# A three-stage transformer forward pass on one core: the routing and the token gather of the expert stage rewritten, the last expert team's down product in pairs, and the final normalisation moved inside that team

## The chip, the cores and the metric

The kernel runs on one core of a Trainium2 chip. The metric is the device time of one execution in microseconds (us), the median of repeated runs. The engines are named as the profile names them: PE (TensorE, matmul; PEld its weight loads), DVE (VectorE), ACT (ScalarE), POOL (GpSimd), SP (SyncE, which here issues almost all DMAs).

## The reference

256 tokens of width 1024, all in float32. Two blocks run one after the other; the change touches only the end of the second.

```python
x = first_block(x, ...)                 # attention / state space mixer, 2 layers, dense FFNs
x = x + mixer(rmsnorm(x, g_mix), ...)   # gated linear attention and block attention
x = x + memory_attention(...)           # cross attention to a memory of 256 tokens
x = x + hier_moe(rmsnorm(x, g_moe), ...)
return rmsnorm(x, g_final)

def hier_moe(h):                        # 32 experts in 4 groups of 8, D_EXPERT = 512
    g_prob = softmax(h @ w_rg + b_rg)               # one group for each token
    p_grp, grp = top_k(g_prob, 1)
    e_in = (h @ w_re + b_re) of that group          # 8 logits
    top_p, top_i = top_k(softmax(e_in), 2)          # two experts for each token
    weights = p_grp * top_p / sum(top_p)
    for each chosen expert e:
        out[token] += ((silu(x @ w_gate[e]) * (x @ w_up[e])) @ w_down[e]) * weight
```

Each expert has 6 MiB of weights (gate and up 1024 x 512, down 512 x 1024), all 32 together 192 MiB, and all of them are read, whatever the routing is.

## The kernel before

Every engine has its own hand-written program (`sync`, `gpsimd`, `scalar`, `tensor`, `vector`), and they meet through semaphores. `X` [128, 2, 1024] holds the residual, with 128 tokens of each of two token blocks (`tb`) on the partitions. All stages before the expert stage split weights and tokens in two parts and take three matmuls for one product (L1259 to L1261); the change doesn't touch them.

**Routing.** After the last output product of the memory attention, DVE adds the residual (`add_residual(5)`). `norm(7)` on PE turns raw `X` by 16 transposes (L1135). DVE and ACT empty two banks each into `HT` (`norm_columns(7)`, L1795 and L718). ACT then squares and sums the rows (`norm_sq(7)`, L710), DVE takes the inverse root in 11 small dependent operations (`rsqrt`, L1766 to L1771) and writes the normed tokens `XN` (L1783). PE makes the 36 router logits from `HT` (L1629). DVE chooses group and experts (L2453 to L2481; a lambda `both` does each step for one token block and then the other), giving `mAS`, which marks the two chosen experts of each token. PE sums `mAS` over tokens (L1638 to L1642), the rank of a token within its expert. DVE meanwhile makes the weights (L2485 to L2493), then from the ranks the slot numbers `mRK` and the number of rounds (L2498 to L2504, semaphore `ranked`). An expert has 32 slots (`SLOTS`); if an expert had more than 32 tokens the whole loop over the experts would be run again (`rounds`; it is 1 here). PE runs filler transposes (`ROUTE_FILLERS`, L1634 and L1754) between these.

**The expert stage.** Experts go in 8 teams of 4. `choose` (DVE, L2516 and L2521) makes `mS`, a 0/1 matrix tokens x (4 experts x 32 slots), and `mSW`, the same with the weights. `gather` (PE, L1649) takes `XN[:, tb, kt::KT]` as the stationary operand, a column stride of 8 elements, and `mS` as the moving one: its 16 matmuls (32 records of the profile, since a float32 matmul has two) give the chosen tokens, turned. ACT and DVE empty four 128-column pieces each into `mGT`. `gate_or_up` (L1697) and `down` (L1718) take a weight slab as the moving operand, and each expert uses 32 columns of the array, so that four run side by side. `turn_hidden` (L1708) turns the hidden values. After `down`, ACT and DVE copy a half each of the result to `mY` (L1101, L2547), and PE scatters it back to the tokens with `mSWT` (L1746, 4 matmuls), and DVE adds to `X` (L2555). Within `team`, PE looks ahead: the gather of the next team stands between `down` and the scatter.

**The transfers.** A piece is 1 MiB, half a matrix of one expert: 24 pieces a team, 192 in all. SP issues them in program order into a ring of 12 slabs. For the first team there are 9 places more (`EXTRA`, buffers that have become free elsewhere), so 21 pieces go out before any expert has been computed. The last of these goes over `HT` and waits for the router logits. Every other piece waits in `put` for the count `piece_used`, which PE raises by 4 each time it has finished a half of gate, up or down (`pay` puts the increment on the next matmul of another phase). The piece after the first 21 therefore waits for the first half of the first team's gate product.

**The end.** `over_teams` runs team 0 (peeled on some engines), a loop, and the last team, then reads the number of rounds from SBUF into a register (`value_load`) and branches. After that ACT squares `X` (`norm_sq(8)`), DVE takes the roots, scales `X` into `XN` (L1783) and multiplies by the gain (L2573), and SP writes each token block out (L600).

## Time and profile before

| what | value |
|---|---|
| median of 3 runs | 1436.96 us (1435.53 to 1438.4) |
| the profiled execution, its own time | 1435.04 us |
| its span, first to last instruction | 1433.3 us |
| mean granted TensorE clock | 0.936 |
| busy in the span: PE, PEld, DVE, ACT, POOL | 1220.0, 965.1, 682.6, 462.5, 27.2 us |
| DMA, mean over the span | 240 GB/s, 343.94 MB |

"Busy" is the time in which an engine executes; a busy engine need not be the one that the end waits for. The expert stage starts near 950 us and runs to the end. Whoever reads this profile has to look at that stage apart from the first two thirds, since its limit is another one.

### The profile page before, as it was taken

What the parts mean: (1) busy time and instruction counts of PE and PEld (TensorE: products, weight loads), DVE (VectorE), ACT (ScalarE), POOL (GpSimd) and SP (SyncE); (2) the same over time, 40 slices, a digit from 0 to 9 for tenths busy, and PEclk for the clock granted to TensorE, in tenths of its full rate; (3) what the DMA queues carried; (4) which work ended last, traced back from release to release, by engine and by line L of the source; (5) the groups of instructions that cost most, each with busy time, mean ns of one, the idle gap of its engine ahead of it and who ended that gap; (6) DMA issues with size and microseconds to landing.
All of it is one profiled execution on the core that took longest, in us unless ns stands there. A gap on an engine that the chain in (4) does not pass through costs nothing. (4 is left out here: it accounts for less than half of the span.)

```text
span 1433.3 us, 19994 instructions
## 1 busy us (share of the span) xinstructions
PE 1220.0 (85%) x8216; PEld 965.1 (67%) x8216; DVE 682.6 (48%) x1012; ACT 462.5 (32%) x588; POOL 27.2 (2%) x83
## 2 busy tenths in 40 slices
PE   6899999999998999999998899989784866748664
PEld 5786999998986999998896897875331332314221
DVE  7987475557777575557355766651110101101012
ACT  6366344325564443325352544411100100101000
POOL 2210000000000000000000000000000000000000
PEclk9899999999999999999995999999997888988897
DMA  9423365554433365556450455876999999999993
GB/s 263 76 83 118 113 227 192 190 189 151 166 109 109 122 226 190 191 176 195 136 177 30 147 177 167 341 300 251 422 420 422 422 422 422 422 421 422 422 421 148
DMA packets 137145, 343.94 MB, mean 240 GB/s; under 512 B 9826, under 2 KB 99036, under 8 KB 112500
## 3 DMA queue, kind: packets, MB, share of 16 engines
q1 hardware_dynamic: 135276, 337.96, 63.0%
q0 software_dynamic: 1696, 4.99, 1.9%
q8 instruction: 50, 0.82, 0.2%
q14 instruction: 19, 0.16, 0.0%
q10 hardware_dynamic: 104, 0.02, 0.0%
HBM read 340.32 MB, written 2.62 MB: 239 GB/s over the span
## 5 line engine op out<-in xcount | busy, mean ns | idle before, releaser
L1259 PE MATMUL ps<-HT_hi,piece_hi 128*128 128x256 f32 x1088 | 310.4, 285 | 7.2 <-DVE HT_lo L1875 4.3
L1884 DVE TENSOR_TENSOR piece_lo<-ring,piece_hi 128x2048 fp32r<-128x2048 f32 x118 | 266.9, 2286 | 87.5 <-ACT piece_hi L766 86.8
L1260 PE MATMUL ps<-HT_lo,piece_hi 128*128 128x256 f32 x1088 | 308.3, 283 | 0.0
L1261 PE MATMUL ps<-HT_hi,piece_lo 128*128 128x256 f32 x1088 | 308.1, 283 | 0.0
L766 ACT ACTIVATE piece_hi<-ring 128x2048 fp32r<-128x2048 f32 x118 | 222.9, 1911 | 195.1 <-PE ps L1261 160.1
L1259 PEld LDWEIGHTS ps<-HT_hi,piece_hi 128*128 128x128 f32 x1088 | 209.0, 192 | 10.7 <-issue 7.8
L1260 PEld LDWEIGHTS ps<-HT_lo,piece_hi 128*128 128x128 f32 x1088 | 209.2, 192 | 0.8
L1261 PEld LDWEIGHTS ps<-HT_hi,piece_lo 128*128 128x128 f32 x1088 | 209.1, 192 | 0.0
L1697 PE MATMUL ps<-ring,arena 128*32 128x512 f32 x992 | 137.7, 712 | 67.9 <-DMA ring<-in_w_exp_up_dram 66.8
L1697 PEld LDWEIGHTS ps<-ring,arena 128*32 128x32 f32 x992 | 36.9, 128 | 162.8 <-issue 161.5
L1718 PE MATMUL ps<-ring,arena 128*32 128x512 f32 x472 | 76.4, 798 | 56.3 <-DMA ring<-in_w_exp_down_dram 56.3
L1718 PEld LDWEIGHTS ps<-ring,arena 128*32 128x32 f32 x472 | 21.5, 139 | 103.0 <-issue 103.0
L2547 DVE COPY arena<-ps 128x512 f32<-128x512 f32 x8 | 5.5, 692 | 143.8 <-PE ps L1718 143.8
L2545 DVE TENSOR_TENSOR arena<-arena,ps 128x512 f32<-128x512 f32 x8 | 5.5, 688 | 141.4 <-PE ps L1697 141.4
L1259 PE MATMUL ps<-piece_hi,HB_hi 128*128 128x512 f32 x176 | 69.7, 396 | 0.0
L1260 PE MATMUL ps<-piece_lo,HB_hi 128*128 128x512 f32 x176 | 69.5, 395 | 0.0
L1261 PE MATMUL ps<-piece_hi,HB_lo 128*128 128x512 f32 x176 | 69.4, 394 | 0.0
L1649 PEld LDWEIGHTS ps<-arena,XN 128*128 128x128 f32 x256 | 61.7, 335 | 8.6 <-issue 8.6
L1649 PE MATMUL ps<-arena,XN 128*128 128x128 f32 x256 | 63.2, 407 | 2.0 <-DVE arena L2521 2.0
L1259 PE MATMUL ps<-piece_hi,HT_hi 128*128 128x256 f32 (+1 forms) x192 | 58.2, 303 | 1.2 <-PE ps L1261 1.2
L1260 PE MATMUL ps<-piece_lo,HT_hi 128*128 128x256 f32 (+1 forms) x192 | 57.7, 301 | 0.0
L1261 PE MATMUL ps<-piece_hi,HT_lo 128*128 128x256 f32 (+1 forms) x192 | 57.7, 301 | 0.0
(451 smaller groups left out, 1711.5 us busy)
## 6 DMA issues: line engine op xcount, KB each, us to landing
ring<-in_w_exp_gate_dram SPq DMA_DIRECT2D x64, 1024.0 KB, 18.6
ring<-in_w_exp_up_dram SPq DMA_DIRECT2D x60, 1024.0 KB, 15.8
ring<-in_w_exp_down_dram SPq DMA_DIRECT2D x59, 1024.0 KB, 15.9
ring<-in_ffn_w_gate_dram SPq DMA_DIRECT2D x22, 1024.0 KB, 5.6
ring<-in_ffn_w_up_dram SPq DMA_DIRECT2D x22, 1024.0 KB, 5.4
ring<-in_ffn_w_down_dram SPq DMA_DIRECT2D x22, 1024.0 KB, 7.3
ring<-in_w_in_dram SPq DMA_DIRECT2D x20, 1024.0 KB, 5.3
ring<-in_odd_w_in_dram SPq DMA_DIRECT2D x12, 1024.0 KB, 5.2
```

The lines of the kernel that those rows point to most:

```text
L766: act.activation(piece_hi[:, h % HI_SLABS, :], ring[:, k % RING, :], ACT.Copy).then_inc(hi_made, 1)
L1259: pe.matmul(out, sh, mh, start=start, stop=False, skip_group_check=True)
L1260: pe.matmul(out, sh, ml, start=False, stop=False, skip_group_check=True)
L1261: return pe.matmul(out, sl, mh, start=False, stop=stop, skip_group_check=True)
L1649: ins = pe.matmul(ps[:, kt // 4, (kt % 4) * P:(kt % 4 + 1) * P], XN[:, tb, kt::KT], mS[:, tb, :], start=(tb == 0), stop=(tb == 1))
L1697: ins = pe.matmul(ps[own, 2 + up, :], mGT[:, kt, own], w[e][:, k4, :], start=(kt == 0), stop=(kt == KT - 1))
L1718: ins = pe.matmul(ps[own, 4 + c, :], mHT[:, 2 * half + f, own], w[e][:, f, c * 512:(c + 1) * 512], start=(half == f == 0), stop=(half == f ...
L1884: ve.tensor_tensor(piece_lo[k % RING][:, :], ring[:, k % RING, :], piece_hi[:, h % HI_SLABS, :].bitcast(F32), ALU.subtract).then_inc(split, 1)
L2545: ve.tensor_tensor(mH, mG, up, ALU.mult).then_inc(m_hid, 1)
L2547: ve.tensor_copy(mY[:, 512:1024], ps[:, 5, :]).then_inc(m_y["v"], 1)
```

## The change

Ahead of the expert stage:

- ACT squares before it empties its half of `norm7`; it also writes `XN` itself, in an order in which the 128 columns that one gather matmul takes lie side by side. DVE no longer writes `XN` at this place.
- The two token blocks' logits are two PSUM tiles of 36 columns, made in turn, as `HT`'s pieces come. The choice on DVE treats both blocks in one instruction where the instruction allows it. The slot numbers count from 1, so that one operation goes.
- `choose` is one operation for `mS` and one for `mSW`. The first `gather` waits for `mS` alone. The number of rounds is counted after the first `choose`.
- The first gather is made in halves: kt 0 to 3, then the first half of gate, then kt 4 to 7. `mGT` is signalled piece by piece. In all teams `gather` reads contiguous columns.
- Fillers go from 60 and 28 to 22 and 6. POOL makes its constants and issues the load of the final gain earlier (after `c_o` instead of after the norm).

At the end:

- `value_load` of the rounds stands ahead of the last team on every engine.
- In the last team, the second `down` half goes by pairs of experts (0, 1 and 2, 3), each with its own waits. In all teams the two column halves are finished one after the other and signalled apart, the scatter goes by column halves.
- Squares, roots, and scaling stand in the last team: ACT squares each block as soon as it is added, DVE multiplies block 1 by the gain meanwhile, and after the roots DVE scales block 0 and ACT block 1. The result lies in `MT`.

```diff
-ROUTE_FILLERS = 60, 28
+ROUTE_FILLERS = 22, 6
@@ over_teams
+                if isinstance(before, int):
+                    eng.wait_ge(ranked, 1)
+                    count = eng.value_load(rounds_i[0:1, :], min_val=1, max_val=T // SLOTS)
                 team(before + (TEAMS - 1), TEAMS - 1, False)
-            one_round(0)
-            eng.wait_ge(ranked, 1)
-            rounds = eng.value_load(rounds_i[0:1, :], min_val=1, max_val=T // SLOTS)
+            rounds = one_round(0)
@@ gpsimd
-            pool.wait_ge(normed, 16)
+            pool.wait_ge(bank_full, full_count("c_o", 1))
@@ scalar
+            norm_sq(7, X)
             norm_columns(7)
-            norm_sq(7, X)
+            act.wait_ge(rt_root, 1)
+            for tb in range(2):
+                act.activation(XN[:, tb, :].rearrange("p (k c) -> p c k", k=KT),
+                               X[:, tb, :].rearrange("p (c k) -> p c k", k=KT), ACT.Copy,
+                               scale=ms[:, 32 + tb:33 + tb]).then_inc(normed, 1)
...
+                else:
+                    for tb in range(2):
+                        act.wait_ge(m_added[tb], g + 2)
+                        ins = act.activation(final_sq[:, tb * D:(tb + 1) * D], X[:, tb, :], ACT.Square, scale=1.0 / 32,
+                                             accum_out=ms[:, 16 + tb:17 + tb])
+                    ins.then_inc(m_sq, TEAMS)
+                    act.wait_ge(m_root, g + 1)
+                    act.activation(result[1], result[1], ACT.Copy, scale=ms[:, 35:36]).then_inc(m_gained, TEAMS)
@@ tensor
+            def gather(g, halves, pay=lambda ins: None):
-                pe.wait_ge(m_sel, g + 1)
-                for kt in range(KT):
-                    for tb in range(2):
-                        ins = pe.matmul(ps[:, kt // 4, (kt % 4) * P:(kt % 4 + 1) * P], XN[:, tb, kt::KT],
-                                        mS[:, tb, :], start=(tb == 0), stop=(tb == 1))
+                pe.wait_ge(m_pick, g * 2 + 2)
+                for half in halves:
+                    for k4 in range(4):
+                        kt = 4 * half + k4
+                        for tb in range(2):
+                            ins = pe.matmul(ps[:, half, k4 * P:(k4 + 1) * P], XN[:, tb, kt * P:(kt + 1) * P],
+                                            mS[:, tb, :], start=(tb == 0), stop=(tb == 1))
...
+                        if half == up == 0 and isinstance(g, int) and g == 0:
+                            gather(g, (1,))
+                            turn(g)
...
+                    for experts in (((0, 1), (2, 3)) if half and not look else (range(TEAM),)):
+                        w = {e: take(2) for e in experts}
                         for c in range(2):
-                            for e in range(TEAM):
...
+                            if half and e == TEAM - 1:
+                                ins.then_inc(m_y_full, 1)
...
-                pe.wait_ge(m_y["a"], g + 1)
-                pe.wait_ge(m_y["v"], g + 1)
-                for tb in range(2):
-                    for half in range(2):
+                for half in range(2):
+                    pe.wait_ge(m_y["av"[half]], g + 1)
...
+                    for tb in range(2):
                         ins = pe.matmul(ps[:, 2 + 2 * tb + half, :], mSWT[:, tb * P:(tb + 1) * P],
@@ vector
                 if not look:
                     ve.wait_ge(m_added[0], g + 2)
                     ve.wait_ge(m_added[1], g + 2)
-                    ve.nop()
+                    ve.tensor_tensor(result[1], X[:, 1, :], gfin, ALU.mult).then_inc(m_finished, TEAMS)
+                    ve.wait_ge(m_sq, g + 1)
+                    ve.wait_ge(m_finished, g * 2 + 2 - TEAMS)
+                    rsqrt(ms[:, 16:18], ms[:, 34:36])
+                    ve.nop().then_inc(m_root, TEAMS)
+                    ve.scalar_tensor_tensor(result[0], X[:, 0, :], ms[:, 34:35], gfin, ALU.mult, ALU.mult)\
+                        .then_inc(m_finished, TEAMS)
```

How the instructions stand on PE where the expert stage begins. The names: `router_w` are the router's weights, `ident` the identity of the fillers and transposes, `arena` holds the choosing matrices, the ranks' operands and the gathered tokens, `ring` is expert weights. Before:

```order
L1629 MATMUL ps<-router_w,HT 128x36 x16
L1634 MATMUL ps<-ident 128x128 x60
L1642 MATMUL ps<-arena 128x32
L1754 MATMUL ps<-ident 128x128 x28
L1649 MATMUL ps<-arena,XN 128x128 x16
L1657 MATMUL ps<-ident,arena 128x128 x2
L1697 MATMUL ps<-ring,arena 32x512 x48
```

After:

```order
L1651 MATMUL ps<-router_w,HT 128x36 x16
L1657 MATMUL ps<-ident 128x128 x22
L1665 MATMUL ps<-arena 128x32
L1790 MATMUL ps<-ident 128x128 x6
L1674 MATMUL ps<-arena,XN 128x128 x8
L1728 MATMUL ps<-ring,arena 32x512 x16
L1674 MATMUL ps<-arena,XN 128x128 x8
L1683 MATMUL ps<-ident,arena 128x128 x2
L1728 MATMUL ps<-ring,arena 32x512 x32
```

The first half of gate (16 matmuls) now has 8 gather matmuls ahead of it instead of 16 and two transposes. (Four of the five rank matmuls are left out in both.)

DVE in the middle of the choice, from the comparison that marks the group to the last operation on `mAS`, all of it on small tiles in `arena`. Before:

```order
L2465 TENSOR_SCALAR arena<-iota,arena 128x4 x2
L2466 TENSOR_SCALAR arena<-arena 128x8 x2
L2468 SCALAR_TENSOR_TENSOR arena<-arena 128x8 x6
L2470 MAX arena<-arena 128x8 x2
L2471 MAX_INDEX arena<-arena 128x8 x2
L2473 TENSOR_TENSOR arena<-arena 128x1 x2
L2474 CAST arena<-arena 128x2 x2
L2476 TENSOR_SCALAR arena<-iota,arena 128x8 x2
L2477 TENSOR_SCALAR arena<-iota,arena 128x8 x2
L2478 TENSOR_TENSOR arena<-arena 128x8 x2
L2481 TENSOR_SCALAR arena<-arena 128x8 x8
```

After:

```order
L2501 TENSOR_TENSOR arena<-iota,arena 128x2x4
L2504 TENSOR_TENSOR arena<-arena 128x2x32
L2506 TENSOR_REDUCE arena<-arena 128x2x8
L2486 MAX arena<-arena 128x8 x2
L2489 MAX_INDEX arena<-arena 128x8 x2
L2508 TENSOR_TENSOR arena<-arena 128x2
L2509 TENSOR_SCALAR arena<-arena 128x2
L2510 CAST arena<-arena 128x2x2
L2518 TENSOR_TENSOR arena<-iota,arena 128x2x16
L2520 TENSOR_TENSOR arena<-arena 128x2x8
L2521 TENSOR_TENSOR arena<-arena 128x64
```

32 instructions have become 13.

DVE at the end of the last team, from the copy of `mY` on (`TENSOR_LOAD` is the read of the number of rounds). Before:

```order
L2547 COPY arena<-ps 128x512
L2555 TENSOR_TENSOR X<-X,ps 128x512 x4
L417 TENSOR_LOAD arena
L417 ISA x2
L418 COMPARE_AND_BRANCH
```

After, where the next eleven rows are the root, as before:

```order
L419 TENSOR_LOAD arena
L419 ISA x2
L2580 TENSOR_TENSOR arena<-arena,ps 128x512
L2583 TENSOR_TENSOR arena<-arena,ps 128x512
L2585 COPY arena<-ps 128x512
L2594 TENSOR_TENSOR X<-X,ps 128x512 x4
L2600 TENSOR_TENSOR MT<-X,final_gain 128x1024
L1802 TENSOR_SCALAR ms<-ms 128x2
```

The read has moved ahead of the last team; the gain's product follows the adds directly.

## Rows read from the trace of the kernel before

**Rows 1.** the page, rate of the DMAs in 40 slices of 35.8 us
```profile
GB/s 263 76 83 118 113 227 192 190 189 151 166 109 109 122 226 190 191 176 195 136 177 30 147 177 167 341 300 251 422 420 422 422 422 422 422 421 422 422 421 148
```

**Rows 2.** stretches of all engines: us, busy times, PEclk, DMA share, GB/s
```profile
960.00:965.00 5.00, 4.33 (x40) 4.10 (x39) 4.69 (x35) 0.00 (x0) 0.00 (x0) 1.00 0.02 7
990.00:1400.00 410.00, 283.74 (x1686) 124.02 (x1682) 46.42 (x102) 31.53 (x63) 0.00 (x0) 0.87 1.01 422
```

**Rows 3.** SP's issues of expert pieces around the gap: start, length, count
```profile
952.41 0.33 SPq L504 DMA_DIRECT2D HT<-in_w_exp_down_dram  x1
980.54 1.29 SPq L517 DMA_DIRECT2D ring<-in_w_exp_down_dram  x3
```

**Rows 4.** PE in order of time, routing and first team
```profile
948.64 3.73 PE L1629 MATMUL ps<-router_w,HT 128*128 128x36 f32 x32 [0.97 <-DVE HT L1795]
952.21 8.41 PE L1634 MATMUL ps<-ident 128*128 128x128 f32 x60
967.66 7.88 PE L1649 MATMUL ps<-arena,XN 128*128 128x128 f32 x32 [1.98 <-DVE arena L2521]
976.84 10.51 PE L1697 MATMUL ps<-ring,arena 128*32 128x512 f32 x96 [1.07 <-ACT arena L1083]
```

**Rows 5.** DVE in order of time, norm, choice, slots
```profile
952.82 1.42 DVE L1783 TENSOR_SCALAR XN<-X,ms 128x1024 f32<-128x1024 f32 x2
...
954.16 0.21 DVE L2455 SCALAR_TENSOR_TENSOR arena<-ps,ms,router_b 128x4 f32<-128x4 f32 x1
...
960.07 1.16 DVE L2481 TENSOR_SCALAR arena<-arena 128x8 f32<-128x8 f32 x8
...
964.68 0.23 DVE L2498 SCALAR_TENSOR_TENSOR arena<-ps,arena 128x64 f32<-128x64 f32 x1
...
966.50 0.49 DVE L2516 TENSOR_TENSOR arena<-arena 128x128 f32<-128x128 f32 x2 [0.62 <-DVE arena L2504]
```

**Rows 6.** ACT in order of time, squares, exponentials, first gathered pieces
```profile
949.48 1.05 ACT L710 ACTIVATE XN<-X 128x1024 f32<-128x1024 f32 x1
...
958.91 0.30 ACT L1077 ACTIVATE arena<-arena 128x4 f32<-128x4 f32 x1 [8.30 <-DVE arena L2473]
...
975.64 1.14 ACT L1083 ACTIVATE arena<-ps,cols 128x128 f32<-128x128 f32 x4 [15.87 <-PE ps L1649]
```

**Rows 7.** a stretch of 1 us in the routing, for the PE clock
```profile
953.00:954.00 1.00, 1.00 (x7) 1.00 (x6) 1.00 (x2) 0.00 (x0) 0.00 (x0) 0.50 1.02 418
```

**Rows 8.** weight loads by form: busy, mean ns
```profile
L1649 PEld LDWEIGHTS ps<-arena,XN 128*128 128x128 f32 x256 | 61.7, 335 | 8.6 <-issue 8.6
...
L1619 PEld LDWEIGHTS ps<-arena 128*128 128x128 f32 x16 | 3.0, 190 | 0.4
```

**Rows 9.** the last two pieces: issues, and us to landing
```profile
L517 SPq DMA_DIRECT2D ring<-in_w_exp_down_dram x2: 429/430/430, 1385.6 to 1386.1; - x2
DMA to landing us min/median/max: 21.1/22.1/23.0
```

**Rows 10.** PE at the end: last down half, scatter
```profile
1399.34 5.34 PE L1718 MATMUL ps<-ring,arena 128*32 128x512 f32 x32 [2.99 <-DMA ring<-in_w_exp_down_dram]
...
1409.27 5.34 PE L1718 MATMUL ps<-ring,arena 128*32 128x512 f32 x32 [4.59 <-DMA ring<-in_w_exp_down_dram]
...
1415.52 3.67 PE L1746 MATMUL ps<-arena 128*128 128x512 f32 x8 [0.91 <-DVE arena L2547]
```

**Rows 11.** the chain that ended last, from the last add on
```profile
1420.60 0.55 DVEq L417
...
1424.09 0.18 DVE ms L1766
...
1426.25 1.43 DVE XN L1783 x2
...
1427.71 1.23 DVE XN L2573
```

**Rows 12.** SP's last issue
```profile
1430.10 0.34 SPq L600 DMA_DIRECT2D out_dram<-XN  x1
```

More of the change, by code:

```diff
@@ L1738, in team @@
                 if look:
-                    gather(g + 1, pay)
+                    gather(g + 1, (0, 1), pay)
                 pe.wait_ge(m_swt, g + 1)
-                pe.wait_ge(m_y["a"], g + 1)
-                pe.wait_ge(m_y["v"], g + 1)
-                for tb in range(2):
-                    for half in range(2):
+                for half in range(2):
+                    pe.wait_ge(m_y["av"[half]], g + 1)
+                    if half and owed:
+                        pe.nop().then_inc(piece_used, TEAM)
+                    for tb in range(2):
                         ins = pe.matmul(ps[:, 2 + 2 * tb + half, :], mSWT[:, tb * P:(tb + 1) * P],
                                         mY[:, half * 512:(half + 1) * 512], start=True, stop=True)
-                        pay(ins)
-                    ins.then_inc(m_out_full, 1)
+                        ins.then_inc(m_out_full, 1)
                 if look:
@@ L2436, in _ @@
             add_residual(5)
+            route = rt.rearrange("p (b c) -> p b c", b=2)
+            o.mark(ve.memset(route[:, :, 36:40], NEG))
             norm_columns(7)
             norm(7, X)
-            rb = full_tile(ve, "router", 0)
-            qs = [rt[:, 128 * tb:128 * tb + 128] for tb in range(2)]
-            def both(*steps):
-                for step in steps:
-                    for q in qs:
-                        o.mark(step(q))
-                ve.wait_ge(v_order, o.count)
@@ new lines, in _ @@
+            logits = route[:, :, 0:32].rearrange("p b (g e) -> p b g e", g=N_GROUPS)
+            in_group, group_is = route[:, :, 96:104], route[:, :, 56:60]
+            for tb in range(2):
+                o.mark(ve.scalar_tensor_tensor(rt[:, 128 * tb:128 * tb + 36], full_tile(ve, "router", tb)[:, 0:36],
+                                               ms[:, 32 + tb:33 + tb], router_b[:, :], ALU.mult, ALU.add))
+            ve.wait_ge(v_order, o.count)
+            ve.nop().then_inc(emptied["v"], 2)
```

241 lines of the change are left out of this document (124 added, 117 removed).

## The prediction, written before the changed kernel ran

> **What bounds the kernel now.** First the rate of the transfers over the whole span [rows 1]. In the first two thirds it goes up and down with the stages. From slice 29 on it stands at 422 GB/s until the end. Ahead of that there is a hole: from 960 to 965 us the DMAs move almost nothing [rows 2], and from 990 to 1400 us they are busy without a break at 422 GB/s, while PE is busy for 284 of 410 us. So the expert stage waits for weights and not for PE.
>
> The hole is explained by SP's issues [rows 3]. The piece over `HT` goes out at 952.41, the next one at 980.54: all 21 places are full, and SP waits for the first half of the first gate product. After that issue 171 pieces of 1.049 MB follow, 179.3 MB, at 422 GB/s 425 us; with a few us of start-up that is 1409, and the last piece lands at 1386.1 + 23.0 = 1409.1 [rows 9], whereupon PE starts at 1409.27 [rows 10]. The end therefore consists of three parts: the time of the issue at 980.54, a stream of fixed length, and what comes after the last landing (1433.3 - 1409.2 = 24.1 us). The change can't shorten the stream. It can move its start and shorten its end.
>
> **The front: from the logits to the issue.** Now [rows 4 to 6]: logits finished at 952.2, DVE first writes `XN` (952.82 to 954.16), chooses until 961.23 (the end of L2481), weights until 964.68, slots until the gather starts at 967.66; gather 7.88 us, turn, `mGT`, gate at 976.84, issue 3.70 us later.
>
> - Start of the choice. The squares no longer wait behind ACT's two banks, and `XN` goes to ACT, so the root is done before the logits are. The choice starts at about 952.3, 1.9 us earlier. Were the root no earlier than now, it would be 952.8; ACT's banks come a bit later, which may hold the logits up by some 0.5 us. Both are in the range.
> - The choice. Now 46 instructions take 7.07 us. After it there are 20: five steps done twice (0.24 to 0.4 us a pair) make 1.8 us, ten single ones make 1.8 us, since a dependent small one costs 2.16/11 = 0.20 (the root from 1424.09 to 1426.25, [rows 11]) and one of 64 columns 0.23 [rows 5]. Together 3.6 us, end at 955.9: 3.5 saved. An operation with a broadcast in four dimensions isn't in these rows; I bound it by 0.16 and 0.49/2 us, which over seven of them is -0.3 and +0.3 us.
> - Exponentials, weights, ranks. ACT's four small instructions (0.30 us the longest, [rows 6]) start at about 955.3 and end at 956.2. Six weight operations are 1.3 us (now 3.45): 957.5. PE's 22 fillers start at 952.2. At the full clock's 3.73/32 = 0.117 us a record [rows 4] they would end at 954.8, at half of it all along at 957.3. At 953 the granted clock is 0.50, the 1.2 GHz level [rows 7], and the 60 fillers now took 8.41 us, 0.14 each, so partly half: I take 956.2. Ten rank records, 1.2 us: 957.4. They just meet the weights.
> - Slots: 0.23 + 0.4 us, since one operation and the counting of rounds go behind the choosers. Gather at 958.35 instead of 967.66: 9.3 us earlier so far.
> - The first gather. Now 32 records take 7.88 us, 0.246 each, with loads of 335 ns; contiguous loads of the same size take 190 ns [rows 8], and the router's 32 records, with contiguous stationary operands, ran at 0.117. Sixteen records by that are 1.9 us (by today's pace 3.9). Then one `mGT` piece, 0.37 us with its wait (four take 1.14, [rows 6]). Gate starts at 960.7 rather than 976.84; this part is 2.35 us where it was 9.18, so 6.8 saved. The other half of gather and the turn, 2.2 us, stand behind the first gate half. They delay only PE, which has slack: ring pieces are used in 3.5 us a group and arrive in 9.9.
>
> The Trainium skill ("TensorE: Matmul & The Clock Gate", section on LDWEIGHTS) says that the time of a weight load depends on its columns alone. By that rule the new layout would change nothing in the gather, and the sum would be 2.0 us smaller. The loads of 335 against 190 ns disagree, with 128 columns in both.
>
> Front: 1.9 + 3.5 + 3.9 + 6.8 = 16.1 us. The issue moves from 980.54 to 964.4. The earlier pieces end near 961 [rows 2, 3], so the hole shrinks from about 20 us to 3.5 and all of the 16.1 passes into the stream. No more than 20 can be had here. SP's queue has no new wait ahead of the issue. POOL's load of the gain (0.5 MB, 1.2 us of transfer) moves to a time when pieces flow; none of them is needed before gate's first half is done, so nothing.
>
> **The tail: from the last landing (called L, 1409.2).** The last two pieces land 2.4 us apart (1385.6 + 21.1, 1386.1 + 23.0, [rows 9]), so the first pair is there at L - 4.9. PE is busy with the other down half until 1404.68 [rows 10].
>
> - Pairs. 96 records, four side by side, took 10.51 us [rows 4], 0.44 a step at full clock; the 32 at 1409.27, after a wait of 4.6 us, took 5.34, partly half clock. A pair has 8 steps: 1404.7 to 1408.2, then L to L + 3.5. The break of 1 us is like the one ahead of 976.84, after which the pace was full. Saved 1.9.
> - Copies lie under the second column half, so the scatter (3.67) follows at once, and one add of about 0.7 is left after it: last add at L + 7.9. Now it ends at 1420.5, L + 11.3. Saved 3.4 with the pairs.
> - Squares: block 0's starts with its own add, block 1's ends 1.6 us after the last add, L + 9.5 (now L + 14.8, since reading the rounds and branching stand between, 1420.60 and 0.55 us of it, and two squares of 1.05 follow). The root's 2.16 stays: L + 11.8 with its waits. The gain's product of block 1 is hidden under the squares.
> - One fused pass, about 1.25 us, on both engines, where 1.43 + 2 x 1.23 stand now [rows 11]; then branch and wait, 0.4: both outputs go at L + 13.4. Now L + 19.8 and L + 20.9 [rows 12], and 3.2 us after the second issue is the end. Two together share the DMAs: 0.35 for the second issue and 0.9 more for its bytes. End at L + 17.9 or so, against 24.1: 6.1 us.
>
> Reading the rounds ahead of the last team costs some 0.8 us on each engine where all of them wait for weights. SP runs far ahead there: its pieces take 21 to 23 us from issue to landing [rows 9].
>
> Sum: 16.1 + 6.1 = 22.2. The profiled execution had 1435.04 us with a span of 1433.3: 1411.1 span, 1412.8 own time. The median lies 1.9 above it: 1436.96 - 22.2 = **1414.8**.
>
> **Rivals.**
>
> - *Half clock where the stream waits.* PE had the half clock at 953 [rows 7]. Should it have it in the first gather and the first gate half, these take 1.9 + 3.5 us more: 1420.2. For it: less filler work stands before. Against it: the gate at 976.84 ran at full pace after a gather and a break.
> - *The gather's pace isn't the load's.* Then the first half takes 3.9: 1416.8.
> - *ACT becomes the routing's bound.* It now squares, empties two banks, writes `XN` with each element 128 apart, and only then comes to the exponentials. At 1.05 us each, as the contiguous pass [rows 6], `XN` is ready at 952.6, 2.7 us before it matters. From 2.4 us each on, each us counts. At four times the price (4.2 each) the exponentials end 3.6 later: 1418.4. No strided write of this size stands in the rows, so this is open. The Trainium skill ("SBUF — State Buffer", in the section on the DMA port swizzle) says that accesses that each go to another 16-byte line pay a penalty. The load of 335 ns above fits that; what ACT pays no row shows.
> - *The front's gain is lost,* since the stream would have another limit behind the hole: only the tail counts, 1430.9. Against it: 422 GB/s without a dip over 410 us.
> - *Nothing changes:* a new wait takes both gains. I see no place that costs 22 us.
> - *Slower: the ring runs dry in every team.* The two halves of the team (columns apart, scatter by halves, waits by piece) hold back `piece_used`. Four pieces give the DMAs 9.9 us, PE needs 5.34 for a group even with a half clock. A release must come about 4.6 us later than now before the DMAs stop. To eat 22.2 + 2.9 us over seven teams it must be 4.6 + 3.6 = 8.2 us later in each. The gather in the loop gets shorter, by up to 4 us, so it speaks against it.
>
> **How the numbers follow.** Forecast 0.63; half clock 0.13; gather's pace 0.07; ACT 0.07; front lost 0.04; nothing 0.03; slower 0.03. The forecast by itself has 1411 to 1418: choice and banks -1 to +2, fillers and ranks -1.3 to +2.3, tail with half clock +3, hole fully closed -3.5. With the half clock and ACT the range is 1410.5 to 1421.5, and some 1 in 10 lie above it. A measurement tells 0.2%, 2.9 us, from no change. Faster 0.94, same 0.03, slower 0.03.
>
> **What would show it.** The first issue after the `HT` piece at about 964.4, and the hole's end with it. The gather's records at 0.12 instead of 0.246 us. `XN` by ACT at 1.05 us each. 422 GB/s through the stream, and the last landing at about 1393. After it some 18 us to the end, with the last 16 down records in 3.5. Wrong it would be if the rate between 970 and 1390 had dips, if the clock at the first gate was 0.5, or if the exponentials came after 957.

## The result and the profile after

| | before | after |
|---|---|---|
| median of 4 runs each | 1436.24 us (1435.06 to 1438.4) | 1411.51 us (1410.73 to 1412.85) |
| span of the profiled execution | 1433.3 | 1409.3 |
| its mean granted clock | 0.936 | 0.929 |

The ratio is 0.9827, with a 95% interval of 0.981 to 0.9844: 24.7 us less, where 22.2 had been forecast. A later group of runs gave 1413.07 us (1410.81 to 1415.3) for the same changed kernel, 21.9 us less than the 1434.92 us of the kernel before in that group. So the difference between two medians wanders by 2.8 us, more than the 2.5 us between forecast and measurement.

First the rate of the DMAs in 40 slices, on the page of the changed kernel, against [rows 1]:

```profile
GB/s 261 83 85 120 92 221 192 191 189 183 146 108 115 118 209 180 183 190 223 158 151 90 120 135 193 297 338 337 421 422 422 422 421 421 423 422 421 423 420 217
```

Then the same in stretches around the hole (length, busy times of PE, PEld, DVE, ACT and POOL, PEclk, DMA share, GB/s), against [rows 2]:

```profile
955.00:960.00 5.00, 4.15 (x37) 3.08 (x40) 2.00 (x9) 1.14 (x4) 0.00 (x0) 1.00 0.41 170
960.00:965.00 5.00, 4.68 (x43) 2.70 (x36) 0.50 (x2) 0.28 (x1) 0.00 (x0) 1.00 0.28 70
965.00:1385.00 420.00, 282.05 (x1786) 103.07 (x1790) 48.27 (x96) 33.51 (x66) 0.00 (x0) 0.83 1.01 422
```

The hole in the stream is still there, but it lasts from about 957 to 963.5 instead of from about 960 to 981. Behind it the stream has the same 422 GB/s, and PE still has a third of its time free (282 of 420 us busy). SP's issues around the hole, in order of time, show why; they answer to [rows 3]:

```profile
950.07 0.33 SPq L510 DMA_DIRECT2D HT<-in_w_exp_down_dram  x1
962.53 1.28 SPq L523 DMA_DIRECT2D ring<-in_w_exp_down_dram  x3
```

From one issue to the next it was 28.1 us and is now 12.5. The program between them, on PE, in order of time, against [rows 4]:

```profile
946.30 3.73 PE L1651 MATMUL ps<-router_w,HT 128*128 128x36 f32 x32 [0.39 <-issue]
949.87 2.60 PE L1657 MATMUL ps<-ident 128*128 128x128 f32 x22
953.97 0.41 PE L1661 MATMUL ps<-arena 128*128 128x32 f32 x2 [1.50 <-DVE arena L2521]
...
956.21 2.02 PE L1674 MATMUL ps<-arena,XN 128*128 128x128 f32 x16 [0.24 <-DVE arena L2556]
958.84 3.64 PE L1728 MATMUL ps<-ring,arena 128*32 128x512 f32 x32 [0.61 <-ACT arena L1095]
962.41 2.05 PE L1674 MATMUL ps<-arena,XN 128*128 128x128 f32 x16
```

On DVE, start of the choice, its end, and the slots, against [rows 5]:

```profile
949.85 0.48 DVE L2495 SCALAR_TENSOR_TENSOR arena<-ps,ms,router_b 128x36 f32<-128x36 f32 x2 [1.42 <-PE ps L1651]
...
953.70 0.22 DVE L2521 TENSOR_TENSOR arena<-arena 128x64 f32<-128x64 f32 x1
...
955.31 0.23 DVE L2535 SCALAR_TENSOR_TENSOR arena<-ps,arena 128x64 f32<-128x64 f32 x1
955.63 0.43 DVE L2556 TENSOR_TENSOR arena<-arena 128x256 f32<-128x256 f32 x1
```

On ACT, `XN` and the first exponential, against [rows 6]:

```profile
948.52 3.94 ACT L1082 ACTIVATE XN<-X,ms 128x1024 f32<-128x1024 f32 x2 [1.59 <-DVEq L1815]
953.20 0.30 ACT L1088 ACTIVATE arena<-arena 128x4 f32<-128x4 f32 x1 [0.74 <-DVEq L2511]
```

The weight loads of the gather, grouped by form (busy time, mean ns), against [rows 8]:

```profile
L1674 PEld LDWEIGHTS ps<-arena,XN 128*128 128x128 f32 x256 | 29.3, 192 | 7.2 <-issue 7.2
```

The end, all engines in order of time with the weight loads left out, against [rows 10] and [rows 12]:

```profile
1391.63 3.63 PE L1753 MATMUL ps<-ring,arena 128*32 128x512 f32 x16 [1.32 <-DMA ring<-in_w_exp_down_dram]
...
1395.18 3.70 PE L1783 MATMUL ps<-arena 128*128 128x512 f32 x8
...
1398.92 0.69 DVE L2594 TENSOR_TENSOR X<-X,ps 128x512 f32<-128x512 f32 x1 [0.17 <-PE ps L1783]
...
1400.79 0.19 ACT L1119 ACTIVATION_READ_ACCUMULATOR HT<-X 128x1 f32 x1
...
1403.38 1.28 DVE L2605 SCALAR_TENSOR_TENSOR MT<-X,ms,final_gain 128x1024 f32<-128x1024 f32 x1 [0.16 <-DVE ms L1807]
1404.96 0.83 SPq L606 DMA_DIRECT2D out_dram<-MT  x2
```

**How to compare two such traces.** The stages ahead of the expert stage are the same program in both, but they don't end at the same time. The first residual add ahead of the routing, on DVE, starts at 941.15 before and at 939.40 after. In the 13 profiled executions of this study it started anywhere from 938.15 to 941.67, and in the two of the changed kernel at 939.40 and 938.15. So I measure the front from the start of that add (called R) to the first issue of a piece after the hole (called the issue), the stream from the issue to the start of the last down products, and the tail from these. "The issue at R + 23.13" means 23.13 us after R. In the table the tail's rows are the time from the start of the last down products to the last add's end, the start of the last root and the end of the span.

| part | before | after | gained | forecast |
|---|---|---|---|---|
| R to the start of the choice | 13.01 | 10.45 | 2.56 | 1.9 |
| the choice (to the end of `mAS`) | 7.07 | 4.07 | 3.00 | 3.5 |
| to the gather (exponentials, weights, ranks, slots) | 6.43 | 2.29 | 4.14 | 3.9 |
| gather to gate | 9.18 | 2.63 | 6.55 | 6.8 |
| gate to the issue | 3.70 | 3.69 | 0.01 | 0 |
| the stream, issue to the last down products | 428.73 | 429.10 | -0.37 | 0 |
| from there to the last add's end | 11.23 | 7.98 | 3.25 | 3.4 |
| ... to the start of the last root | 14.82 | 9.46 | 5.36 | 5.3 |
| ... to the end | 24.03 | 17.67 | 6.36 | 6.1 |

Front 16.26, stream -0.37 and tail 6.36 make 22.25. R's 1.75 us are the rest of the 24.0 us between the spans (1433.3 - 1409.3).

### The profile page after: what moved, and what is told of

It reads as the page before. It is cut to its first block, busy times and chain, and to the rows that moved or that the text cites. A ratio compares the mean times of both kernels' runs of the same rounds, so it can differ in the third digit from the quotient of the medians.

```text
span 1409.3 us, 19857 instructions
## 1 busy us (share of the span) xinstructions
PE 1192.3 (85%) x8156; PEld 926.1 (66%) x8156; DVE 674.5 (48%) x948; ACT 467.7 (33%) x591; POOL 28.9 (2%) x83
## 4 chain that ended last, share of the span: by engine, by line
PE 59%; DMA 23%; DVE 9%; ACT 4%; issue 3%; SPq 2%; POOL 0%; DVEq 0%; ACTq 0%; POOLq 0%
PE ps L1279 15%; PE ps L1280 14%; PE ps L1281 14%; DMA ring<-in_w_exp_down_dram 11%; DMA ring<-in_w_exp_up_dram 11%; PE ps L1728 4%; PE ps L1753 3%; DVE piece_lo L1923 1%; SPq L523 1%; PE ps L1195 1%; DVE arena L2271 1%; ACT piece_hi L772 1%; PE ps L1383 1%; PE ps L1155 1%; DVE arena L1872 1%
## 5 line engine op out<-in xcount | busy, mean ns | idle before, releaser
L1728 PE MATMUL ps<-ring,arena 128*32 128x512 f32 x992 | 149.6, 759 | 85.5 <-DMA ring<-in_w_exp_up_dram 64.3
L1728 PEld LDWEIGHTS ps<-ring,arena 128*32 128x32 f32 x992 | 40.9, 134 | 187.1 <-issue 186.6
L1753 PE MATMUL ps<-ring,arena 128*32 128x512 f32 x472 | 80.3, 800 | 47.0 <-DMA ring<-in_w_exp_down_dram 47.0
L1753 PEld LDWEIGHTS ps<-ring,arena 128*32 128x32 f32 x472 | 21.5, 142 | 98.1 <-issue 98.1
L1110 ACT ACTIVATE arena<-ps 128x512 f32<-128x512 f32 x8 | 4.8, 597 | 162.2 <-PE ps L1742 162.2
L1944 DVE TENSOR_TENSOR arena<-ps,arena 128x512 f32<-128x512 f32 x22 | 15.2, 692 | 84.4 <-PE ps L1281 84.3
```

Source lines behind the costliest of these rows:

```text
L1728: ins = pe.matmul(ps[own, 2 + up, :], mGT[:, kt, own], w[e][:, k4, :], start=(kt == 0), stop=(kt == KT - 1))
L1753: ins = pe.matmul(ps[own, 4 + c, :], mHT[:, 2 * half + f, own], w[e][:, f, c * 512:(c + 1) * 512], start=(half == f == 0), stop=(half == f ...
L1944: ve.tensor_tensor(by_token(G), by_token(gate), roots[1 + 2 * layer][1].unsqueeze(1).to_broadcast([P, 2, T]), ALU.mult).then_inc(gate_scal ...
```

## The experiments

Each group of runs had its own runs of the kernel before, with medians of 1436.42 (first four kernels), 1436.36 (next four) and 1434.92 (last three). Each ratio is against these. Edits are shown against the changed kernel, except the first. Where the text speaks of the changed kernel's 1411.51 us or of R + 23.13, it means the runs and the profile of the result. The changed kernel's own medians differ by 1.6 us from group to group, so for smaller effects the profiles carry the argument.

**1. The tail alone (tail_only).** The kernel before, with the change's edits behind the last landing only: pairs, copies and scatter by halves, `value_load` ahead of the last team, squares and gain inside it. For instance:

```diff
-            one_round(0)
-            eng.wait_ge(ranked, 1)
-            rounds = eng.value_load(rounds_i[0:1, :], min_val=1, max_val=T // SLOTS)
+            rounds = one_round(0)
@@ scalar, and so in the other places of the end
-            norm_sq(8, X)
+            act.nop().then_inc(fin[1], 1)
```

> The kernel before with only the end of the change: the rounds read ahead of the last team, the last down half in pairs, scatter by column halves, squares and scaling in the last team. Theory A (fixed stream between a front and a tail, which add): no change up to the last landing, then 17.7 us to the end where the kernel before has 24.0, so 6.3 us faster, near 1430. Theory B (the end gains only because the front also moved, or the extra reads and waits in the loop cost something): less than 4 us faster, and a rate under 422 GB/s in the stream.

Measured: 1429.59 us (1428.8 to 1431.43), ratio 0.9949 [0.9932, 0.9966], 6.8 us less than its runs of before. In its profile R is at 941.20 and the issue at R + 41.1, against R + 39.4 in the kernel before, since the first gate product took 12.20 us against 10.51 in [rows 4]: the clock was at 0.50 from 977 to 980. From the issue to the end of the last add are 437.1 us, as in the changed kernel (1399.61 - 962.53). From the issue to the end it is 447.4 where the kernel before has 452.8 and the changed one 446.8. So the tail is worth 5.4 us by the profiles and 6.8 by the medians (forecast 6.1), as theory A said, and the rest belongs to the front.

**2. Gather with the old stride (strided).**

```diff
-                act.activation(XN[:, tb, :].rearrange("p (k c) -> p c k", k=KT),
-                               X[:, tb, :].rearrange("p (c k) -> p c k", k=KT), ACT.Copy,
+                act.activation(XN[:, tb, :], X[:, tb, :], ACT.Copy,
@@ tensor, gather
-                            ins = pe.matmul(ps[:, half, k4 * P:(k4 + 1) * P], XN[:, tb, kt * P:(kt + 1) * P],
+                            ins = pe.matmul(ps[:, half, k4 * P:(k4 + 1) * P], XN[:, tb, kt::KT],
```

> The changed kernel, with XN in its old order: ACT writes it contiguously, and the gather takes every eighth column as its stationary operand. Theory A (a weight load with a stride of 32 bytes is slower, and the front passes one to one into the end): 0.246 us a record, the first gather half 3.9 instead of 2.0 us, the issue after the gap 2 us later, the time 2 us longer; ACT's two passes at 1.05 instead of 1.97 us win nothing. Theory B (load time depends on columns alone): no change of the gather. Theory C (ACT's pass is what the routing waits for): faster, by up to 1.8 us.

Measured: 1418.67 us (1417.07 to 1420.74), ratio 0.9876 [0.986, 0.9893], 7.2 us over the changed kernel. PE in order of time around the first gather:

```profile
957.69 4.04 PE L1673 MATMUL ps<-arena,XN 128*128 128x128 f32 x16 [0.24 <-DVE arena L2555]
962.34 5.34 PE L1727 MATMUL ps<-ring,arena 128*32 128x512 f32 x32 [0.61 <-ACT arena L1094]
```

Its weight loads by form, its `XN` on ACT, and two stretches (columns as above):

```profile
L1673 PEld LDWEIGHTS ps<-arena,XN 128*128 128x128 f32 x256 | 61.8, 335 | 7.2 <-issue 7.2
```

```profile
950.04 2.19 ACT L1082 ACTIVATE XN<-X,ms 128x1024 f32<-128x1024 f32 x2 [1.62 <-DVEq L1814]
```

```profile
1000.00:1005.00 5.00, 4.88 (x23) 1.91 (x25) 4.43 (x10) 1.27 (x2) 0.00 (x0) 1.00 1.01 423
1005.00:1010.00 5.00, 5.00 (x52) 1.62 (x48) 0.10 (x1) 0.40 (x1) 0.00 (x0) 1.00 0.67 211
```

The same 16 records take 4.04 us with the stride and 2.02 without it, and in the gather nothing but the operand's address pattern differs. That is what theory A said, and it rules out theory B. The rest of the 7.2 us A did not foresee. The first half of gate took 5.34 instead of 3.64, at a granted clock of 0.62 and 0.52 between 962 and 966, and the stream had a dip to 211 GB/s at 1005 to 1010. My reading of the dip is that PE came late to the next release of ring places: it was busy for 19.9 of the 20 us from 990 to 1010. The strided gather of the next team, 32 records in 7.91 us, can't be the whole reason, for the kernel before has the same gather in the same place and no dip:

```profile
1000.15 7.90 PE L1649 MATMUL ps<-arena,XN 128*128 128x128 f32 x32
```

```profile
1015.00:1020.00 5.00, 3.71 (x36) 0.91 (x28) 0.59 (x1) 0.60 (x1) 0.00 (x0) 1.00 1.02 423
1020.00:1025.00 5.00, 3.43 (x20) 1.06 (x24) 0.10 (x1) 0.00 (x0) 0.00 (x0) 0.66 1.01 421
```

From the issue to the start of the second team's gate there are 31.1 us before (1011.64 - 980.54), 29.9 in the changed kernel (992.44 - 962.53) and 36.1 in strided (1003.80 - 967.73). What is new in strided is that the second half of the first gather, 4.10 us with the stride, now also stands behind the issue. So the dip goes with the split and the stride together; this is argued from the traces, not tried by itself. The sum is closed: R 1.48 later, gather 2.02, gate half 1.70, stream 2.14 and tail 0.06 make the 7.4 between the spans. Of the 5.9 us without R, the strided loads ahead of the issue are a third; the stream's 2.1 came later, and whether the stride has any part in the clock's fall at gate isn't shown. (Tail_only, whose gather is strided too, had the fall at the same place, the kernel before had one earlier, at 970, during its gather.) The contiguous write by ACT, 2.19 us where it was 3.94, won nothing, so theory C falls: ACT then waited 2.46 us for DVE instead of 0.74.

**3. The first gather whole (whole).**

```diff
-                if isinstance(g, int):
-                    gather(g, (0,))
-                else:
-                    gather(g, (0, 1))
-                    turn(g)
+                gather(g, (0, 1))
+                turn(g)
@@ team
-                        if half == up == 0 and isinstance(g, int) and g == 0:
-                            gather(g, (1,))
-                            turn(g)
```

> The changed kernel, with the first gather made as a whole (16 matmuls and the turn) ahead of the first gate half. Theory A: the first gate half ends 2.2 to 2.4 us later, the DMA gap is longer by that, the time 2.3 us longer. Theory B (the split is hidden by the wait for the first gathered pieces): under 1 us.

Measured: 1414.36 us (1413.56 to 1415.57), ratio 0.9845 [0.9829, 0.9862]. The issue comes at R + 24.47 instead of 23.13. So the halves are worth 1.34 us: 1.79 for the 16 other records (3.81 us for 32, 2.02 for 16) and 0.14 for the turn's transposes, less the wait of 0.61 us for ACT ahead of gate, which these records cover. That lies between the theories (2.2 to 2.4, and under 1): A left out the covered wait. The median is 2.85 us higher, but of the 3.4 us between the profiled spans 2.27 are R, at 941.67.

**4. A delay ahead of the gather (delay).** `ROUTE_FILLERS = 22, 92` instead of 22, 6.

> The changed kernel with 86 more filler transposes (92 instead of 6) between the ranks and the first gather, at 0.117 us each 10.1 us of pure delay on PE. Theory A (one to one): the issue after the gap 10 us later, the last landing 10 us later, the tail as it is, 9.8 us longer (some 0.3 us of the fillers were hidden). Theory B (slack in the stream takes part of it): less than 8 us.

Measured: 1421.98 us (1420.31 to 1424.67), ratio 0.9903 [0.9886, 0.992]. The issue is at R + 33.70, 10.57 later than in the changed kernel, and the median is 10.5 higher. From the issue to the end are 446.9 us, against 446.8. Theory A holds: the delay passes to the end one to one. Its size isn't the fillers' alone, since the clock was at 0.50 from 954 to 957.

**5 and 6. Fillers (fill_none, fill_old).** `ROUTE_FILLERS = 0, 0`, and `60, 28` as before.

> The changed kernel without any filler transposes in the routing. Theory A (the fillers hold the PE clock through the first gather and gate, and cost nothing, since PE waits for VectorE at the ranks anyway): the clock falls to the 1.2 GHz level somewhere from the ranks to the first gate, the issue after the gap comes 2 to 5 us later. Theory B (they do nothing, the later work is dense enough): gate at 19.4 us after the first residual add, as now, and no change of the time within 1 us.

> The changed kernel with the old number of fillers, 60 and 28. By 0.117 us each at full clock the 60 end at 7.0 us instead of 2.6 after the router's matmuls; PE waits 1.5 us for VectorE there now, so the ranks come 2.9 us later. The 28 instead of 6 take 2.6 us more, of which 0.2 are a wait now; the choosers are 2.9 us later too. Together 5.2 to 5.5 us later at the issue and in the time. If the clock is at half for a part, up to 8 us.

Measured: without fillers 1415.81 us (1415.75 to 1416.05), ratio 0.9858 [0.9841, 0.9874], issue at R + 25.90. With the old ones 1419.03 (1415.49 to 1420.41), ratio 0.9884 [0.9867, 0.99], issue at R + 27.43. Both cost, for opposite reasons. Without fillers the issue comes 2.8 us later, within theory A's 2 to 5. With the old ones it comes 4.3 us later, where 5.2 to 5.5 were expected: 60 fillers took 6.6 us from start to start of what follows, 0.110 each, not 0.117. PE without fillers, a stretch of it (PE alone: busy, PEclk, DMA share, GB/s) and the gather:

```profile
954.00:956.00 2.00, 0.00 (x0) 0.50 1.02 430
```

```profile
956.09 0.64 PE L1661 MATMUL ps<-arena 128*128 128x32 f32 x2 [3.94 <-DVE arena L2521]
...
959.37 3.76 PE L1674 MATMUL ps<-arena,XN 128*128 128x128 f32 x16 [0.93 <-DVE arena L2556]
```

PE waits 3.94 us for the choice, the clock falls to 0.50, the 1.2 GHz level, and ranks and gather run at that level. With 60 and 28 fillers PE has no wait at all from the router's products to the gather and the clock stays at 1.00 from 945 to 970 in this execution, but the fillers are themselves in the way:

```profile
950.07 6.75 PE L1657 MATMUL ps<-ident 128*128 128x128 f32 x60
...
957.69 3.25 PE L1790 MATMUL ps<-ident 128*128 128x128 f32 x28
```

The profiled execution was the fastest of the four; what made the other three 2.5 to 4.9 us longer no trace shows.

**7. No pairs (no_pairs).**

```diff
-                    for experts in (((0, 1), (2, 3)) if half and not look else (range(TEAM),)):
+                    for experts in (range(TEAM),):
```

> The changed kernel, the last down half in one group of four experts. Theory A: PE stands idle for 5 us ahead of the last landing and then does 32 records instead of 16, with the clock at half for a part: 5.3 instead of 3.6 us, last add 1.7 to 2 us later, the time the same. Theory B (pairs win by an earlier first column half alone): under 0.5 us, since both have 8 steps after the last landing.

Measured: 1413.77 us (1413.04 to 1417.31), ratio 0.9851 [0.9834, 0.9867]. The last down half in one piece:

```profile
1392.92 4.92 PE L1753 MATMUL ps<-ring,arena 128*32 128x512 f32 x32 [3.46 <-DMA ring<-in_w_exp_down_dram]
```

The last add ends 9.27 us after the start of these products instead of 7.98, and the end is 18.98 behind instead of 17.67: the pairs are worth 1.3 us. They don't save steps: at the full clock 32 records of a down half took 3.64 us (the first half, in the profile of whole), and the 16 of the last pair take 3.63, since both have eight steps one after the other. What they save is the clock. Without pairs PE waits 3.46 us for the landing, and the clock is at 0.50 from 1393 to 1395; with them it waits 1.32 us, and the clock is at 1.00 from 1392 to 1395. So theory A had the reason, with a price of 1.7 to 2 us that was too high, and B left the clock out. Another 1.16 us of its profiled span come from the front, where the clock fell at 955 in this execution.

**8. The number of rounds read late (late_rounds).**

```diff
             def one_round(before):
...
+                team(before + (TEAMS - 1), TEAMS - 1, False)
                 if isinstance(before, int):
                     eng.wait_ge(ranked, 1)
                     count = eng.value_load(rounds_i[0:1, :], min_val=1, max_val=T // SLOTS)
-                team(before + (TEAMS - 1), TEAMS - 1, False)
```

> The changed kernel, with the rounds read behind the last team, as before. The read was 0.55 us in the chain before, with its issue some 0.9: the outputs are issued 0.8 to 1.0 us later relative to the last landing, and nothing else moves. Rival: reading it in the loop's last turn costs PE time ahead of the last team, then this kernel is the same or faster.

Measured: 1414.97 us (1413.75 to 1415.32), ratio 0.985 [0.9834, 0.9867]. The last add ends at the same 7.98, but the outputs are issued 14.24 us after the start of the last products instead of 13.33. The read behind the team costs 0.9 us, all of it between the writing of the result and its issue, as expected; the rival falls. The rest of the median's difference is not the read's: in the profiled execution the clock fell at 951, during the router's products, so that the issue came at R + 24.67, and R itself was at 940.93.

**9. The changed kernel again (after_again).**

> The changed kernel once more, unchanged, as the measure for the other kernels of this group. Theory A (my account of the profiled pair): the change is worth 22.6 us (16.3 ahead of the stream's restart, 6.4 behind the stream), and the remaining 1.75 us of the two spans' difference lies ahead of the residual add and is scatter between executions. Then the residual add starts anywhere from 938 to 942 us in this execution, the wait of 960 us lasts to 23.1 us after it, the tail after the last down projection's start is the same to 0.1 us, and the median lies within 1411 to 1414. Theory B: the 1.75 us are a gain of the change by some effect on the earlier part: then the residual add starts at 939.4 again, within 0.5 us, where the kernels of the groups before had 938.3 to 941.7.

Measured: 1413.07 us (1410.81 to 1415.3), ratio 0.9853 [0.9836, 0.9869]. R is at 938.15, so theory B falls: the 1.75 us of the profiled pair are scatter ahead of the change. The kernels that share the changed front have R from 938.15 to 941.67, on both sides of the 941.15 before. But A's 23.1 us to the issue were not met either; it was 24.29. PE of this execution, and a stretch of it (PE alone):

```profile
948.62 2.60 PE L1657 MATMUL ps<-ident 128*128 128x128 f32 x22
952.73 0.41 PE L1661 MATMUL ps<-arena 128*128 128x32 f32 x2 [1.51 <-DVE arena L2521]
...
954.01 1.52 PE L1790 MATMUL ps<-ident 128*128 128x128 f32 x6
955.32 2.81 PE L1674 MATMUL ps<-arena,XN 128*128 128x128 f32 x16
```

```profile
954.00:956.00 2.00, 2.00 (x11) 0.50 0.87 360
```

The instructions are the same, behind the same wait of 1.5 us as in the first profile, yet here the clock went to 0.50 and cost 1.16 us. What decides between the two no trace shows.

**10. More fillers, only as many as fit (fill_34).** `ROUTE_FILLERS = 34, 6`.

> 34 filling matmuls instead of 22 ahead of the ranks, everything else as in the changed kernel. The ranks waited 1.50 us for VectorE there, and a filler took 0.117 us (22 in 2.60): 12 more take 1.4 us and end just as VectorE has the picks ready. Theory A (the time is VectorE's and the fillers only fill): issue after the gap and median within 0.3 us of the changed kernel's. Theory B (some executions of the changed kernel lose the clock in the gap, and more filling holds it): the median falls by up to 1.5 us, to about 1410, and its spread narrows. Against both: if the fillers ran at 0.19 us each, as they would at half the clock, they would end 2.3 us late and the median would be 1 to 2 us above.

Measured: 1411.36 us (1410.98 to 1413.2), ratio 0.984 [0.9826, 0.9854]. PE:

```profile
950.25 3.91 PE L1657 MATMUL ps<-ident 128*128 128x128 f32 x34
954.36 0.41 PE L1661 MATMUL ps<-arena 128*128 128x32 f32 x2 [0.20 <-DVE arena L2521]
```

The fillers end as VectorE has the marks ready, the clock stays at 1.00 from 945 to 970, and the issue comes at R + 23.13, as in the better of the changed kernel's two profiles: theory A's figure. (At half clock a filler costs more than the 0.19 us of the expectation: in late_rounds the 22 took 4.93 us, 0.22 each.) Against the changed kernel of the same group the median is 1.7 us lower; against its eight runs of both groups (median 1412.2) 0.8 us. The intervals overlap, so this version is no worse in these runs, and that it is better isn't shown.

**11. ACT's banks ahead of its squares (cols_first).**

```diff
-            norm_sq(7, X)
             norm_columns(7)
+            norm_sq(7, X)
```

> ScalarE empties its banks of turned columns before it squares, as in the kernel before; the rest is the changed kernel. The root and the strided write of XN then come later on ScalarE by the time of the bank copies, about 1 to 2 us, and the two writes last 3.94 us. In the changed kernel ScalarE ended them 0.74 us before VectorE had the arguments of the exponentials. Theory A (the routing is VectorE's; ScalarE has 0.74 us to spare): the exponentials start (delay minus 0.7) later, and with the later root of the logits' scaling the issue after the gap moves by about 1 to 1.7 us, median 1412.5 to 1413.5. Theory B (the order of the two jobs on ScalarE decides nothing, the router's products came first anyway): issue and median within 0.3 us.

Measured: 1415.88 us (1415.08 to 1416.9), ratio 0.9865 [0.985, 0.9881], issue at R + 27.01, 3.9 later: more than either theory gave. ACT and PE:

```profile
953.18 3.83 ACT L1082 ACTIVATE XN<-X,ms 128x1024 f32<-128x1024 f32 x2 [2.26 <-DVEq L1815]
956.82 0.25 ACT L1088 ACTIVATE arena<-arena 128x4 f32<-128x4 f32 x1
```

```profile
957.30 0.64 PE L1661 MATMUL ps<-arena 128*128 128x32 f32 x2 [3.06 <-DVE arena L2521]
...
960.77 3.39 PE L1674 MATMUL ps<-arena,XN 128*128 128x128 f32 x16
```

The root comes later and the choice starts 1.28 us later (first `max` at R + 12.35 instead of 11.07). Now the exponentials follow `XN` without a wait, and DVE waited 0.41 us for them instead of 0.17. But that didn't reach the end, for with the weights made DVE still had to wait for the ranks:

```profile
959.68 0.22 DVE L2535 SCALAR_TENSOR_TENSOR arena<-ps,arena 128x64 f32<-128x64 f32 x1 [0.77 <-PE ps L1665]
```

The other 2.6 us are PE: after a wait of 3.06 us the clock is at 0.50 from 957 until past 963, and from the start of the ranks to the start of gate it takes 7.48 us instead of 4.87. Of theory A's 1 to 1.7 us there are 1.28, by the later root and none by ACT's own length; what A left out was the clock.

## Why the prediction was right

The mechanism was right: the end is a front, a stream of fixed length, and a tail, and the two ends were shortened by about what was said. That the sum of the parts came out at 22.25 against 22.2 is partly luck: the four front terms were off by +0.7, -0.5, +0.2 and -0.25 us, and the misses cancel.

**The limit.** The end is the issue plus a constant. In the eight profiles of kernels which leave the stream and the tail alone (after, after_again, whole, delay, fill_none, fill_old, fill_34, cols_first) the span minus the time of the issue lies between 446.6 and 446.9 us, while the issue itself moves from 962.4 to 972.0. That confirms the step on which all rested, and rules out the rival that the front's gain is lost. Of the hole some 6.5 us are left, where the prediction had 3.5: it took the start of the hole as 961 and left it there, but transfers ended near 960 before and end near 957 now, since R came 1.75 us and the logits another 0.6 us earlier. A front gain of 10 us more would not have passed whole into the stream.

**Start of the choice.** 2.56 us instead of 1.9. I had let the logits end as before; they came 0.6 us earlier, since PE waited 0.39 us ahead of them and not 0.97 [rows 4]. The root was done 1.4 us before the logits (DVE's wait of 1.42), so it had the cover that the prediction gave it.

**Choice.** 3.00 instead of 3.5. Twenty instructions took 4.07 us and not 3.6. By start to start, the five steps done twice were 1.97 us (forecast 1.8), the ten single ones 2.10 (1.8): two of them on 64 columns took 0.26 and 0.30 with their gap, and the step behind the cast waited 0.15 us for it. The bound of +0.3 us for the broadcasts held.

**Exponentials to slots.** 4.14 instead of 3.9. The fillers had the full clock (2.60 us, not the 4.0 that I chose between the bounds of 2.6 and 5.1), so PE was not late but waited 1.50 us for the marks. This miss cost nothing, since ranks and weights ended together at 955.3, and the weights alone (1.25 us, forecast 1.3) would have held the slots until then.

**Gather.** 6.55 instead of 6.8. Its 16 records took 2.02 (forecast 1.9), and the first piece on ACT and its waits 0.61 (forecast 0.37). Experiment 2 shows that the pace belongs to the load: 335 ns with a column stride of eight elements, 192 without, with 128 columns both times. The rival "the gather's pace isn't the load's" falls with it, and so does the sum by the rule of the Trainium skill ("TensorE: Matmul & The Clock Gate", section on LDWEIGHTS), in which columns alone count.

**The tail.** 6.36 instead of 6.1; the tail alone gave 5.4 to 6.8. Inside it the pairs were over-sized: 5.34 - 3.63 = 1.7 us against the kernel before, and 1.3 against experiment 7, not 1.9. All of it is the granted clock (experiment 7): in one piece the 32 records took 5.34 us in one execution and 4.92 in the other, and 3.64 where the clock was full. Against the kernel before the rest of the 3.25 us is 1.5 for copies and scatter by halves, as set.

**The rivals.** *Half clock where the stream waits* got 13 in 100 and a price of 5.4 us. It is the one that was nearest to being seen. Its price was set too high: at half clock the first gather took 3.76 us instead of 2.02 (fill_none, forecast 1.9 more), but the first gate half 5.34 instead of 3.64 (strided), 1.7 us more and not 3.5, and no execution had both in full. Of the seven profiled executions with the changed kernel's fillers (after, after_again, whole, strided, delay, no_pairs, late_rounds) the clock fell during the router's products or between them and the first gather in four, and in a fifth (strided) during the first gate half. The price in the two of the changed kernel was 0 and 1.16 us, since the level came back before gate. So it explains scatter of 1 to 2 us and not another result. *ACT becomes the bound:* the strided write took 1.97 us a block, not 1.05, below the 2.4 from which I let it count. It ended 0.74 us ahead of need, and when it was pushed past that (experiment 11) DVE's wait for it grew by 0.24 us, which the wait for the ranks hid. The Trainium skill ("SBUF — State Buffer", in the section on the DMA port swizzle) lets accesses that each go to another 16-byte line pay a penalty; the 1.97 us against 1.10 in order agree with that. *The ring runs dry* was not seen in the changed kernel, but once in strided, for 2.1 us. The prediction had no place for it there, since it let the second half of the first gather delay only PE; with contiguous loads (2.05 us) it did, with strided ones (4.10 us) it no longer did.

**The size.** Forecast 22.2 against 22.25 by parts; the median moved by 24.7, and the range of 1410.5 to 1421.5 held it near its lower end. The surplus is not the change's: 1.75 us of the profiled pair are R, and in the later group the same two kernels were 21.9 us apart. Why the identical stages ahead end at times 3.5 us apart stays open.

## What to carry to other kernels

Where a kernel is bound by a stream of weights, look for the one issue that the stream restarts from, and treat everything ahead of it as the critical path. What stands behind it, up to the last landing, is free only as long as places are released in time: strided lost 2.1 us there. Measure two versions from a landmark just ahead of the change, not by their spans, or the scatter of the earlier stages goes into the account. Size filler work by the wait that it is to fill (here 1.5 us, 12 transposes of 0.117): more stands in the way, as fill_old shows. That less makes the clock fall is shown for none at all (fill_none, one profile); with 22 it fell in some executions and not in others.

## What the hardware showed that was not expected

- A weight load of 128 x 128 whose columns stand eight elements apart took 335 ns, a contiguous one 192, and the float32 products behind it 0.25 against 0.12 to 0.13 us a record.
- ACT's pass over 128 x 1024 took 1.97 us with the elements written 128 apart (3.94 for two) and 1.10 when written in order (2.19 for two).
- The clock fell to 0.50 behind a wait of PE of 1.5 us in some executions and not in others of the same instructions. Behind waits of 3.06 and 3.94 us it fell in both cases seen.
- Fillers, which are transposes of the identity, don't surely hold the clock. In fill_old, and in fill_34 with a wait of 0.20 us, it stayed at 1.00. But in the kernel before it was at 0.50 from 953 to 956, while PE ran the 60 fillers without a break ([rows 4], [rows 7]), and in late_rounds it fell during the router's products. The level also comes back under fillers: before it was 1.00 again from 957, with nothing but fillers run since 952.2, and in delay from 958, with only fillers since 954.1.
- A group of 32 down records, four experts side by side, and a pair's 16 took the same 3.6 us at the full clock (3.64 and 3.63); only the clock made one piece dearer, 4.92 us.
